# Entry of the in-projection: x also laid out by channel, u formed on VectorE instead of transposed on TensorE

## The chip, the cores and the metric

The kernel runs on one core of one Trainium2 chip. Its time is the device time of one launch in microseconds (us), from inputs in device memory to the output there. Below, TensorE is PE in the rows, VectorE is DVE, ScalarE is ACT, GpSimd is POOL and SyncE is SP; SyncE issues most of the DMAs.

## The reference, cut to what matters

Two transformer blocks run one after the other on 1024 tokens of width 1024, all in float32. What the change touches is the first line of the first block: the RMS norm of the input and the product with `w_in`.

```python
def rms_norm(x, g):
    xf = x.astype(jnp.float32)
    y = xf * lax.rsqrt(jnp.mean(xf * xf, axis=-1, keepdims=True) + EPS)
    return (y * g.astype(jnp.float32)).astype(x.dtype)
...
        u = rms_norm(h, attn_pre_norm[i])
        c_q, c_kv, k_rope, m_q, m_k, m_v, m_o, m_i, m_f = split_cols(u @ w_in[i], IN_SIZES)
```

All that follows (latent attention, mLSTM, output projection, gated feed-forward, the second block's pool mixer and layer norm) reads this projection, directly or in turn.

## The kernel before, in words

Five programs, one for each engine, are written out by hand. Each engine runs its own in order and waits on semaphores; there is no scheduler. The order of the code is the order of the work.

A product with full float32 accuracy is made of three matmuls in a faster format (`three`, L1316 and on; the matmul itself is L1325). Each operand is split into a rounded part `_hi` and the rest `_lo`, and hi x hi, hi x lo and lo x hi are summed in PSUM.

The projection wants u with the channels on the partitions: `u_hi` and `u_lo`, 128 partitions x 8 channel blocks (k) x 1024 tokens. x lies in memory by token. The entry brings it there in token tiles of 128 (t = 0 to 7), and the first weight tile is multiplied in token quarters of 256 (q = 0 to 3, two tiles each):

- SyncE loads the rows of tiles 0 and 1, the first weight tile in two halves, then tiles 2 to 7, then small tables, and later the second weight tile.
- ScalarE (`x_norm`, L1939) squares a tile with a running sum and takes the root, which gives the deviation of each token (`row_sd` counts tiles).
- TensorE spreads the norm weight over all partitions at the very start (L1359: `ones` times `gain_row` into PSUM banks 2 and 3) and warms up with 14 transposes (L1362). VectorE copies the spread weight to `pre_gain` (L2644).
- VectorE (`x_scale`, L2629) takes the reciprocal and scales the tile by token and by channel, in place (`rows_ready`).
- TensorE (`x_transposed`, L1335) transposes the tile's eight channel blocks into two PSUM banks of 4 to 7 (`rows_full`). A tile from 2 on first waits until the banks' last user is through.
- ScalarE (`u_rounded`, L1948) writes `u_hi` from PSUM (`rows_hi`), and VectorE (`u_low`, L2635) writes `u_lo` as the difference (`rows_split`).
- TensorE multiplies quarter q once `rows_split` has reached 4q + 4: for each of two column halves m of the weight tile 24 matmuls of 256 columns. In quarter 0 the matmuls with the weights' high part come first (L1371, L1372), those with the low part later (L1378), since `w_lo` is still being made by GpSimd and VectorE. Between these groups stand the transposes of the next quarter's two tiles.

After the last group `in_tile(1, ...)` goes on with the second weight tile in 128x512 matmuls. From there on the kernel streams weights: SyncE loads, GpSimd, ScalarE and VectorE split and combine, TensorE multiplies.

## Time and profile before

| | us |
|---|---|
| median of 3 runs | 1821.05 (1820.62 to 1822.2) |
| the profiled execution's own time | 1821.14 |
| its span in the trace | 1819.3 |
| TensorE busy | 1795.2 |
| VectorE busy | 1405.3 |
| ScalarE busy | 686.0 |
| GpSimd busy | 1079.0 |

Times in a trace are counted from the start of the span. The page gives the busy time of each engine and the granted clock of TensorE in 40 slices; the windows give the same for any stretch. A timeline lists instructions with start, length and, in brackets, the idle time in front and what ended it. Matmuls overlap, so the length of a single one is longer than its share of a run of them: the share is read from the starts. L12 is line 12 of the kernel before.

### The profile page before, as it was taken

Reading aid. Unit: us, or ns where it says so; the run is one execution under the profiler, and the core shown is the slowest. Engines: PE = TensorE matmul, PEld = TensorE weight load, DVE = VectorE, ACT = ScalarE, POOL = GpSimd, SP = SyncE. Lnnn points to the kernel's source line nnn. Section 1 sums busy time; section 2 is a strip of 40 time slices with the busy share of each in tenths; the row PEclk is TensorE's granted clock in tenths of the full one; section 3 lists DMA queues with packets and bytes.
Section 4 is the critical chain, followed back from the end, with each engine's and each line's share of the span. In section 5 each row is a group of like instructions: output and inputs, shape, how many; then the busy total and the mean of one; then the engine's idle time right before and its main releaser. Section 6 shows DMA issues by size and latency. Waiting matters only on the chain.

```text
span 1819.3 us, 22566 instructions
## 1 busy us (share of the span) xinstructions
PE 1795.2 (99%) x8522; PEld 1500.2 (82%) x8522; DVE 1405.3 (77%) x1614; ACT 686.0 (38%) x1202; POOL 1079.0 (59%) x748
## 2 busy tenths in 40 slices
PE   8999999999999999999999999999999999999998
PEld 8888888888888888888888887888888888888877
DVE  7879866666596757676599989668888875698897
ACT  5555577852321111111243333415433343333313
POOL 4056632170259988888778876732665465567554
PEclk9999999999999999999999999999999999999999
DMA  6252310032313323143374631112332232943122
GB/s 161 84 162 56 112 46 17 17 128 93 106 45 104 116 81 116 58 151 116 104 275 176 231 128 47 47 47 105 127 116 104 105 130 79 356 176 106 73 100 93
DMA packets 126575, 204.44 MB, mean 112 GB/s; under 512 B 31986, under 2 KB 87922, under 8 KB 123011
## 3 DMA queue, kind: packets, MB, share of 16 engines
q1 hardware_dynamic: 126434, 202.93, 32.7%
q8 instruction: 68, 1.11, 0.3%
q14 instruction: 39, 0.32, 0.1%
q10 hardware_dynamic: 34, 0.07, 0.0%
HBM read 149.42 MB, written 53.04 MB: 111 GB/s over the span
## 4 chain that ended last, share of the span: by engine, by line
PE 68%; DVE 5%; POOL 3%; issue 3%; ACT 1%; DMA 0%; DVEq 0%; SPq 0%; POOLq 0%
PE ps L1325 60%; PE ps L1652 1%; PE ps L1654 1%; PE ps L1653 1%; POOL ring_lo L1188 1%; POOL ring_hi L1187 1%; DVE y L3511 1%; PE ps L1890 1%; PE ps L1891 1%; PE ps L1892 1%; DVE y L3504 0%; DVE xs_lo L3338 0%; DVE y L3233 0%; POOL y L1244 0%; PE ps L1767 0%
## 5 line engine op out<-in xcount | busy, mean ns | idle before, releaser
L1325 PE MATMUL ps<-f_hi,ring_hi 128*128 128x512 f32 x384 | 149.7, 390 | 1.2 <-POOL ring_lo L1188 1.2
L1325 PE MATMUL ps<-f_lo,ring_hi 128*128 128x512 f32 x384 | 149.4, 389 | 0.0
L1325 PE MATMUL ps<-f_hi,ring_lo 128*128 128x512 f32 x384 | 149.4, 389 | 0.0
L1259 POOL TENSOR_TENSOR ring_lo<-w_sum,ring_hi 128x512 fp32r<-128x512 f32 x60 | 94.8, 1590 | 51.2 <-ACT ring_hi L2447 51.1
L1325 PE MATMUL ps<-d_w_hi,d_hid_hi 128*128 128x512 f32 x312 | 121.7, 390 | 1.6 <-DVE y L3233 1.3
L1188 POOL TENSOR_TENSOR ring_lo<-w_sum,ring_hi 128x512 fp32r<-128x512 f32 x80 | 117.9, 1474 | 6.7
L1325 PE MATMUL ps<-d_w_hi,d_hid_lo 128*128 128x512 f32 x312 | 121.4, 389 | 0.0
L1325 PE MATMUL ps<-d_w_lo,d_hid_hi 128*128 128x512 f32 x312 | 121.4, 389 | 0.0
L2324 ACT ACTIVATE f_copy<-ps 128x512 f32<-128x512 f32 x60 | 35.3, 596 | 220.2 <-PE ps L1325 201.3
L1325 PE MATMUL ps<-xs_hi,ring_hi 128*128 128x512 f32 x256 | 100.0, 391 | 1.4 <-DVE xs_lo L3338 1.4
L1325 PE MATMUL ps<-xs_hi,ring_lo 128*128 128x512 f32 x256 | 99.6, 389 | 0.0
L1325 PE MATMUL ps<-xs_lo,ring_hi 128*128 128x512 f32 x256 | 99.6, 389 | 0.0
L1325 PE MATMUL ps<-fs_hi,ring_hi 128*128 128x512 f32 x240 | 93.5, 389 | 0.0
L1325 PE MATMUL ps<-fs_lo,ring_hi 128*128 128x512 f32 x240 | 93.4, 389 | 0.0
L1325 PE MATMUL ps<-fs_hi,ring_lo 128*128 128x512 f32 x240 | 93.4, 389 | 0.0
L1187 POOL TENSOR_SCALAR ring_hi<-w_sum 128x512 fp32r<-128x512 f32 x80 | 71.8, 898 | 32.5 <-PE ps L1325 32.0
L1187 POOL TENSOR_SCALAR ring_hi<-stage 128x512 fp32r<-128x512 f32 x38 | 33.4, 878 | 89.1 <-PE ps L1654 83.3
L1325 PEld LDWEIGHTS ps<-f_hi,ring_hi 128*128 128x128 f32 x384 | 72.1, 188 | 16.8 <-POOL ring_lo L1188 1.9
L1325 PEld LDWEIGHTS ps<-f_hi,ring_lo 128*128 128x128 f32 x384 | 72.1, 188 | 15.1
L1325 PEld LDWEIGHTS ps<-f_lo,ring_hi 128*128 128x128 f32 x384 | 72.1, 188 | 14.8
L1073 POOL TENSOR_TENSOR w_lo<-stage,w_hi 128x1024 fp32r<-128x1024 f32 x32 | 80.5, 2515 | 2.7
L1259 POOL TENSOR_TENSOR ring_lo<-stage,ring_hi 128x512 fp32r<-128x512 f32 x24 | 35.1, 1465 | 76.4 <-ACT ring_hi L2447 76.4
(542 smaller groups left out, 5792.9 us busy)
## 6 DMA issues: line engine op xcount, KB each, us to landing
d_raw<-hid_rows SPq DMA_DIRECT2D x37, 512.0 KB, 4.5
stage<-in_w_up SPq DMA_DIRECT2D x22, 512.0 KB, 4.5
wd_raw<-in_w_down SPq DMA_DIRECT2D x22, 512.0 KB, 5.6
raw_w<-in_w_gate SPq DMA_DIRECT2D x20, 512.0 KB, 4.9
stage<-in_pool_w_in SPq DMA_DIRECT2D x16, 512.0 KB, 4.9
raw_w<-in_pool_w_in SPq DMA_DIRECT2D x16, 512.0 KB, 4.8
m_rows<-u_row SPq DMA_DIRECT2D x16, 512.0 KB, 2.6
z_rows<-z_buf SPq DMA_DIRECT2D x8, 1024.0 KB, 4.1
```

Source lines behind the costliest of these rows:

```text
L1073: g.tensor_tensor(lo, stage[:, h, :], hi.bitcast(F32), ALU.subtract).then_inc(parted[h], 1)
L1187: pool_hi.do(pool, g.tensor_scalar(view(hi), src, 1.0, 0.0, ALU.mult, ALU.add))
L1188: g.tensor_tensor(view(lo), src, view(hi).bitcast(F32), ALU.subtract).then_inc(w_split, 1)
L1259: g.tensor_tensor(as_blocks(lo, src), src, as_blocks(hi, src).bitcast(F32), ALU.subtract).then_inc(w_split, 1)
L1325: last = mm(out_ap, l, r, start=(start and j == 0), stop=(stop and j == n - 1), skip_group_check=onto)
L1652: mm(o, l_hi, w_hi[s][:, c:c + HALF], start=(k == 0), stop=False)
L1653: mm(o, l_hi, w_lo[s][:, c:c + HALF], start=False, stop=False)
L1654: last = mm(o, l_lo, w_hi[s][:, c:c + HALF], start=False, stop=(k == 7))
L1890: mm(ps[:, m, :], w_hi[1][:, c:c + P], x_h, start=(k == 0), stop=False)
L1891: mm(ps[:, m, :], w_hi[1][:, c:c + P], x_l, start=False, stop=False)
L1892: last = mm(ps[:, m, :], w_lo[1][:, c:c + P], x_h, start=False, stop=(k == 3))
L2324: f(copies[:, j, :], ps[:, bank0 + bank_of[o], :], ACT.Copy).then_inc(prod_copied, 1)
```

## The change

x of the last three quarters of the tokens is handed to the kernel a second time, as `x_t`: 128 partitions (channel within its block) x 8 columns of the norm weight, and then for each quarter 8 channel blocks x 256 tokens, 3.1 MB in all. SyncE loads it in three parts, each behind the rows of its quarter, which now come as one load of two tiles. The rows are still loaded, because the sum of squares is taken over them.

For tiles 0 and 1 nothing changes but the source of the norm weight: `x_scale` reads it from PSUM in two halves of 512, and `pre_gain` and its copy are gone.

For quarters 1 to 3 nothing is transposed. VectorE (`spread_row`) makes a diagonal matrix of the reciprocals of one tile, two of them for a quarter. TensorE (`spread_columns`) multiplies it by `ones`, which puts the reciprocal of each of 256 tokens on all partitions, into the first 256 columns of PSUM bank 3. VectorE (`u_quarter`) then forms u in PSUM banks 4 to 7 with eight instructions, one a channel block: `x_t` times the norm weight's column times bank 3. ScalarE's rounding and VectorE's subtraction read it from there as before, two channel blocks of 256 tokens a time. Since bank 3 is taken, the results of quarters 2 and 3 lie in banks 2 and 3 in another order, and `c_q_raw` is copied out accordingly.

```diff
@@ -144,9 +144,11 @@
 
 
         x_nat = at("x_nat", [P, TB, D], C)
-        pre_gain = at("pre_gain", [P, D], E)
+        x_t = at("x_t", [P, KD + 3 * KD * (S // 4)], B)
+        gain_cols = x_t[:, 0:KD]
+        spread = at("spread", [P, 6 * P], E)
         gain_row = at("gain_row", [P, D], Z)
-        junk0 = at("junk0", [P, D], B + 16 * KB)
+        junk0 = at("junk0", [P, D], B + 25 * KB)
         u_hi = at("u_hi", [P, KD, S], A, F32R)
         u_lo = at("u_lo", [P, KD, S], A + 32 * KB, F32R)
@@ -652,6 +654,10 @@
             return (1 + t + 2 * e if t < 2 else 2 * t + e + 1)
 
 
+        def spread_bank():
+
+            return ps[:, 3, 0:QT]
+
         def sp_program(sp):
             def load(t, sources):
@@ -677,8 +683,11 @@
                 x_rows(t)
             for h in range(2):
                 sp.dma_start(view[h], src[h]).then_inc(staged[h], 16)
-            for t in range(2, TB):
-                x_rows(t)
+            for q in range(1, 4):
+                rows = a["x"][0, 2 * q * P:2 * (q + 1) * P, :].rearrange("(t p) n -> p t n", p=P)
+                sp.dma_start(x_nat[:, 2 * q:2 * q + 2, :], rows).then_inc(rows_in[2 * q], 16)
+                c0, c1 = KD * QT * (q - 1) + KD if q > 1 else 0, KD * QT * q + KD
+                sp.dma_start(x_t[:, c0:c1], a["x_t"][:, c0:c1]).then_inc(rows_in[2 * q + 1], 16)
 
             for j in range(4):
@@ -1334,10 +1343,8 @@
 
             def x_transposed(t):
                 pe.wait_ge(rows_ready, t + 1)
-                if t >= 2:
-                    pe.wait_ge(rows_split, 2 * (t - 2) + 2)
                 for k in range(KD):
-                    b, c = 4 + 2 * (t % 2) + k // 4, (k % 4) * P
+                    b, c = 4 + 2 * t + k // 4, (k % 4) * P
                     last = tr(ps[:, b, c:c + P], x_nat[:, t, k * P:(k + 1) * P], ident[:])
                     if k % 4 == 3:
@@ -1363,6 +1370,12 @@
             for t in range(2):
                 x_transposed(t)
             QUARTER = S // 4
+
+            def spread_columns(q):
+                pe.wait_ge(rows_ready, 2 * q + 2)
+                cs = slice((q - 1) * QUARTER, q * QUARTER)
+                mm(spread_bank(), ones[:], spread[:, cs], start=True, stop=True).then_inc(gain_spread, 1)
+
             pe.wait_ge(rows_split, 4)
             pe.wait_ge(pool_hi.sem, 2)
             for m in range(2):
@@ -1370,26 +1383,23 @@
                     w_h = wcols(0, k, m)[0]
                     mm(ps[:, m, 0:QUARTER], w_h, u_hi[:, k, 0:QUARTER], start=(k == 0), stop=False)
                     mm(ps[:, m, 0:QUARTER], w_h, u_lo[:, k, 0:QUARTER], start=False, stop=False)
-            x_transposed(2)
-            x_transposed(3)
             tile_ready(0)
             for m in range(2):
                 for k in range(KD):
                     mm(ps[:, m, 0:QUARTER], wcols(0, k, m)[1], u_hi[:, k, 0:QUARTER], start=False, stop=(k == KD - 1))
+                if m == 0:
+                    spread_columns(1)
             for j in range(2, 8):
                 q, m = j // 2, j % 2
                 pe.wait_ge(rows_split, 4 * q + 4)
-                if j == 4:
-                    pe.wait_ge(gain_spread, 3)
                 ts = slice(q * QUARTER, (q + 1) * QUARTER)
-                c = (q % 2) * QUARTER
-                last = three(ps[:, 2 * (q // 2) + m, c:c + QUARTER],
+                b, c = (m, QUARTER) if q == 1 else (q, m * QUARTER)
+                last = three(ps[:, b, c:c + QUARTER],
                              [(*wcols(0, k, m), u_hi[:, k, ts], u_lo[:, k, ts]) for k in range(KD)])
                 if q % 2 == 1:
                     last.then_inc(in_full, 1)
                 if m == 0 and q < 3:
-                    x_transposed(2 * q + 2)
-                    x_transposed(2 * q + 3)
+                    spread_columns(q + 1)
             in_tile(1, 1, 4, 4, first=True)
 
...
@@ -1949,7 +1959,13 @@
                 for j in range(2):
                     act.wait_ge(rows_full, 2 * t + j + 1)
                     f(u_hi[:, 4 * j:4 * j + 4, t * P:(t + 1) * P],
-                      ps[:, 4 + 2 * (t % 2) + j, :].rearrange("p (k n) -> p k n", k=4),
+                      ps[:, 4 + 2 * t + j, :].rearrange("p (k n) -> p k n", k=4),
+                      ACT.Copy).then_inc(rows_hi, 1)
+
+            def u_quarter_rounded(q):
+                for j in range(4):
+                    act.wait_ge(rows_full, 4 * q + j + 1)
+                    f(u_hi[:, 2 * j:2 * j + 2, q * QT:(q + 1) * QT], ps[:, 4 + j, :].rearrange("p (k n) -> p k n", k=2),
                       ACT.Copy).then_inc(rows_hi, 1)
 
             x_norm(0)
@@ -1959,15 +1975,12 @@
             x_norm(2)
             x_norm(3)
             x_norm(4)
-            u_rounded(2)
-            u_rounded(3)
             x_norm(5)
+            u_quarter_rounded(1)
             x_norm(6)
-            u_rounded(4)
-            u_rounded(5)
             x_norm(7)
-            u_rounded(6)
-            u_rounded(7)
+            u_quarter_rounded(2)
+            u_quarter_rounded(3)
 
             act.wait_ge(early_dve, 1)
...
@@ -2629,39 +2644,70 @@
             def x_scale(t):
                 dve.wait_ge(row_sd, t + 1)
                 own.do(dve, v.reciprocal(stat_c[:, t:t + 1], stat_b[:, t:t + 1]))
-                v.scalar_tensor_tensor(x_nat[:, t, :], x_nat[:, t, :], stat_c[:, t:t + 1], pre_gain[:],
-                                       ALU.mult, ALU.mult).then_inc(rows_ready, 1)
+                for n in range(2):
+                    dve.wait_ge(gain_spread, n + 1)
+                    ins = v.scalar_tensor_tensor(x_nat[:, t, half(n)], x_nat[:, t, half(n)], stat_c[:, t:t + 1], ps[:, 2 + n, :],
+                                                 ALU.mult, ALU.mult)
+                    if n == 0:
+                        own.mark(ins)
+                own.wait(dve)
+                ins.then_inc(rows_ready, 1)
 
             def u_low(t):
                 for j in range(2):
                     dve.wait_ge(rows_hi, 2 * t + j + 1)
                     ts = slice(t * P, (t + 1) * P)
                     v.tensor_tensor(u_lo[:, 4 * j:4 * j + 4, ts],
-                                    ps[:, 4 + 2 * (t % 2) + j, :].rearrange("p (k n) -> p k n", k=4),
+                                    ps[:, 4 + 2 * t + j, :].rearrange("p (k n) -> p k n", k=4),
                                     u_hi[:, 4 * j:4 * j + 4, ts].bitcast(F32), ALU.subtract).then_inc(rows_split, 1)
 
-            dve.wait_ge(gain_spread, 2)
-            v.tensor_copy(pre_gain[:], psf[:, 2 * HALF:4 * HALF]).then_inc(gain_spread, 1)
-            dve.wait_ge(gain_spread, 3)
+            def spread_row(t):
+                dve.wait_ge(row_sd, t + 1)
+                own.do(dve, v.reciprocal(stat_c[:, t:t + 1], stat_b[:, t:t + 1]))
+                v.tensor_scalar(spread[:, (t - 2) * P:(t - 1) * P], ident[:], stat_c[:, t:t + 1], None,
+                                ALU.mult).then_inc(rows_ready, 1)
+
+            def u_quarter(q):
+                dve.wait_ge(rows_in[2 * q + 1], 16)
+                dve.wait_ge(gain_spread, 2 + q)
+                dve.wait_ge(rows_split, 4 * q)
+                for k in range(KD):
+                    c = KD + (KD * (q - 1) + k) * QT
+                    ins = v.scalar_tensor_tensor(ps[:, 4 + k // 2, (k % 2) * QT:(k % 2 + 1) * QT], x_t[:, c:c + QT],
+                                                 gain_cols[:, k:k + 1], spread_bank(), ALU.mult, ALU.mult)
+                    if k % 2:
+                        ins.then_inc(rows_full, 1)
+                    else:
+                        own.mark(ins)
+                own.wait(dve)
+
+            def u_quarter_low(q):
+                ts = slice(q * QT, (q + 1) * QT)
+                for j in range(4):
+                    dve.wait_ge(rows_hi, 4 * q + j + 1)
+                    v.tensor_tensor(u_lo[:, 2 * j:2 * j + 2, ts], ps[:, 4 + j, :].rearrange("p (k n) -> p k n", k=2),
+                                    u_hi[:, 2 * j:2 * j + 2, ts].bitcast(F32), ALU.subtract).then_inc(rows_split, 1)
+
             x_scale(0)
             x_scale(1)
             u_low(0)
             u_low(1)
-            x_scale(2)
-            x_scale(3)
+            dve.wait_ge(consts, N_CONSTS)
+            spread_row(2)
+            spread_row(3)
             dve.wait_ge(pool_hi.sem, 2)
             w0 = slice(1024, 2048)
             v.tensor_tensor(w_lo[0][:, w0], stage[:, 1, :], w_hi[0][:, w0].bitcast(F32), ALU.subtract).then_inc(parted[1], 1)
-            x_scale(4)
-            u_low(2)
-            u_low(3)
-            x_scale(5)
-            x_scale(6)
-            u_low(4)
-            u_low(5)
-            x_scale(7)
-            u_low(6)
-            u_low(7)
+            u_quarter(1)
+            spread_row(4)
+            spread_row(5)
+            u_quarter_low(1)
+            u_quarter(2)
+            spread_row(6)
+            spread_row(7)
+            u_quarter_low(2)
+            u_quarter(3)
+            u_quarter_low(3)
 
             def u_rows(k):
                 if k == 3:
@@ -3626,6 +3672,8 @@
     given = {name: _np.ascontiguousarray(inputs[name]) for name in _INS}
 
     freq = _np.float32(10000.0) ** (-_np.arange(0, ROPE, 2, dtype=_np.float32) / _np.float32(ROPE))
+    x_cols = given["x"][0].T.reshape(KD, P, 4, S // 4)[:, :, 1:].transpose(1, 2, 0, 3).reshape(P, -1)
+    given["x_t"] = _np.ascontiguousarray(_np.concatenate([given["attn_pre_norm"][0].reshape(KD, P).T, x_cols], axis=1))
     given["p"] = _np.ascontiguousarray(given["p"][0, 0].T)
     given["inv_freq"] = _np.ascontiguousarray(_np.tile(freq.astype(_np.float32), 4)[:, None])
     for name, x in given.items():
```

In the rows below `w_hi_49` and `w_lo_54` are the two parts of the first weight tile. TensorE, around the low-weight part of quarter 0, before (`x_nat` rows are transposes of tiles 2 and 3; L1378 the low-weight matmuls; L1325 quarter 1):

```order
L1341 MATMUL ps<-ident,x_nat 128x128 [waits rows_split,rows_ready]
L1341 MATMUL ps<-ident,x_nat 128x128 x7
L1341 MATMUL ps<-ident,x_nat 128x128 [waits rows_split,rows_ready]
L1341 MATMUL ps<-ident,x_nat 128x128 x7
L1378 MATMUL ps<-u_hi,w_lo_54 128x256 [waits parted1,parted0]
L1378 MATMUL ps<-u_hi,w_lo_54 128x256 x15
L1325 MATMUL ps<-u_hi,w_hi_49 128x256 [waits rows_split]
```

and now:

```order
L1389 MATMUL ps<-u_hi,w_lo_54 128x256 [waits parted1,parted0]
L1389 MATMUL ps<-u_hi,w_lo_54 128x256 x7
L1377 MATMUL ps<-spread,ones 128x256 [waits rows_ready]
L1389 MATMUL ps<-u_hi,w_lo_54 128x256 x8
L1334 MATMUL ps<-u_hi,w_hi_49 128x256 [waits rows_split]
L1334 MATMUL ps<-u_lo,w_hi_49 128x256
L1334 MATMUL ps<-u_hi,w_lo_54 128x256
```

The 16 transposes are gone from in front of the low-weight matmuls, and one matmul with the diagonals of tiles 2 and 3 stands in the middle of them. Then TensorE, between the two column halves of quarter 1, before:

```order
L1325 MATMUL ps<-u_lo,w_hi_49 128x256
L1325 MATMUL ps<-u_hi,w_lo_54 128x256
L1341 MATMUL ps<-ident,x_nat 128x128 [waits rows_split,rows_ready]
L1341 MATMUL ps<-ident,x_nat 128x128 x7
L1341 MATMUL ps<-ident,x_nat 128x128 [waits rows_split,rows_ready]
L1341 MATMUL ps<-ident,x_nat 128x128 x7
L1325 MATMUL ps<-u_hi,w_hi_49 128x256 [waits rows_split]
L1325 MATMUL ps<-u_lo,w_hi_49 128x256
```

and now:

```order
L1334 MATMUL ps<-u_lo,w_hi_49 128x256
L1334 MATMUL ps<-u_hi,w_lo_54 128x256
L1377 MATMUL ps<-spread,ones 128x256 [waits rows_ready]
L1334 MATMUL ps<-u_hi,w_hi_49 128x256 [waits rows_split]
L1334 MATMUL ps<-u_lo,w_hi_49 128x256
L1334 MATMUL ps<-u_hi,w_lo_54 128x256
```

The transposes of tiles 4 and 5 have made room for one matmul; it stands behind the 24 matmuls of quarter 1's first half. The same holds for quarter 2. VectorE from the low part of the first weights on, before:

```order
L2654 TENSOR_TENSOR w_lo_54<-stage,w_hi_49 128x1024 [waits pool_hi]
L2631 RECIPROCAL cols<-cols 128x1 [waits row_sd]
L2632 SCALAR_TENSOR_TENSOR x_nat<-x_nat,cols,pre_gain 128x1024 [waits dve_own]
L2639 TENSOR_TENSOR u_lo<-ps,u_hi 128x4x128 [waits rows_hi] x4
L2631 RECIPROCAL cols<-cols 128x1 [waits row_sd]
L2632 SCALAR_TENSOR_TENSOR x_nat<-x_nat,cols,pre_gain 128x1024 [waits dve_own]
L2631 RECIPROCAL cols<-cols 128x1 [waits row_sd]
L2632 SCALAR_TENSOR_TENSOR x_nat<-x_nat,cols,pre_gain 128x1024 [waits dve_own]
L2639 TENSOR_TENSOR u_lo<-ps,u_hi 128x4x128 [waits rows_hi] x4
```

and now:

```order
L2700 TENSOR_TENSOR w_lo_54<-stage,w_hi_49 128x1024 [waits pool_hi]
L2676 SCALAR_TENSOR_TENSOR ps<-x_t,ps 128x256 [waits rows_split,gain_spread,rows_in3]
L2676 SCALAR_TENSOR_TENSOR ps<-x_t,ps 128x256 x7
L2666 RECIPROCAL cols<-cols 128x1 [waits row_sd,dve_own]
L2667 TENSOR_SCALAR spread<-ident,cols 128x128 [waits dve_own]
L2666 RECIPROCAL cols<-cols 128x1 [waits row_sd]
L2667 TENSOR_SCALAR spread<-ident,cols 128x128 [waits dve_own]
L2688 TENSOR_TENSOR u_lo<-ps,u_hi 128x2x256 [waits rows_hi] x4
L2676 SCALAR_TENSOR_TENSOR ps<-x_t,ps 128x256 [waits rows_split,gain_spread,rows_in5]
```

Where two scalings of a tile stood ahead of the four subtractions of a quarter, now stand eight products that wait for `gain_spread` (TensorE's matmul with the diagonals) and the diagonals of the quarter after.

## Rows read from the trace of the kernel before

**Rows 1.** The page, part 1: busy us and share of the span.
```profile
PE 1795.2 (99%) x8522; PEld 1500.2 (82%) x8522; DVE 1405.3 (77%) x1614; ACT 686.0 (38%) x1202; POOL 1079.0 (59%) x748
```

**Rows 2.** Windows, a stretch each; columns in the row that begins core 0.
```profile
core 0: us, PE busy (x) PEld busy (x) DVE busy (x) ACT busy (x) POOL busy (x), PEclk, DMA share, GB/s
...
12.00:14.00 2.00, 0.43 (x5) 0.19 (x3) 1.89 (x3) 2.00 (x4) 1.92 (x2) 1.00 1.02 418
43.00:225.00 182.00, 182.00 (x805) 150.69 (x805) 159.51 (x148) 97.23 (x131) 80.68 (x48) 1.00 0.33 100
1813.00:1815.00 2.00, 0.00 (x0) 0.00 (x0) 1.93 (x4) 1.24 (x2) 0.00 (x0) 1.00 0.65 262
1815.00:1817.00 2.00, 0.00 (x0) 0.00 (x0) 1.62 (x4) 0.20 (x2) 0.00 (x0) 0.96 0.00 0
1817.00:1819.30 2.30, 0.00 (x0) 0.00 (x0) 0.00 (x0) 0.00 (x0) 0.00 (x0) 0.50 0.61 228
```

**Rows 3.** Waits of TensorE, 22.3 to 225 us: total, times, longest.
```profile
PE ps L1325 <- DVE u_lo L2639: 0.5, 1, 0.5
```

**Rows 4.** Timeline of TensorE: start us, length, instructions, idle before.
```profile
2.72 3.75 PE L1359 MATMUL ps<-gain_row,ones 1*128 1x512 f32 x4 [2.72 <-POOL causal L1055]
6.40 3.25 PE L1362 MATMUL ps<-ident 128*128 128x128 f32 x14
9.44 2.94 PE L1341 MATMUL ps<-ident,x_nat 128*128 128x128 f32 x16
13.95 0.39 PE L1371 MATMUL ps<-u_hi,w_hi 128*128 128x256 f32 x1 [1.57 <-DVE u_lo L2639]
...
17.88 1.91 PE L1341 MATMUL ps<-ident,x_nat 128*128 128x128 f32 x16
19.55 2.15 PE L1378 MATMUL ps<-u_hi,w_lo 128*128 128x256 f32 x16
22.22 0.39 PE L1325 MATMUL ps<-u_hi,w_hi 128*128 128x256 f32 x1 [0.53 <-DVE u_lo L2639]
...
25.20 1.91 PE L1341 MATMUL ps<-ident,x_nat 128*128 128x128 f32 x16
...
43.07 0.40 PE L1325 MATMUL ps<-u_hi,w_hi 128*128 128x512 f32 x1
```

**Rows 5.** Timeline of VectorE.
```profile
14.36 0.17 DVE L2631 RECIPROCAL cols<-cols 128x1 f32<-128x1 f32 x1 [0.47 <-ACT cols L1942]
...
17.16 1.22 DVE L2654 TENSOR_TENSOR w_lo<-stage,w_hi 128x1024 fp32r<-128x1024 f32 x1
...
26.72 2.47 DVE L2639 TENSOR_TENSOR u_lo<-ps,u_hi 128x512 fp32r<-128x512 f32 x4
```

**Rows 6.** Timeline of ScalarE.
```profile
11.37 1.70 ACT L1951 ACTIVATE u_hi<-ps 128x512 fp32r<-128x512 f32 x3 [0.23 <-PE ps L1341]
```

**Rows 7.** Groups of VectorE: count, busy us, mean ns, idle before.
```profile
L2639 DVE TENSOR_TENSOR u_lo<-ps,u_hi 128x512 fp32r<-128x512 f32 x16 | 10.0, 682 | 3.4 <-ACT u_hi L1951 3.3
L2671 DVE TENSOR_TENSOR u_whole<-u_hi,u_lo 128x512 f32<-128x512 f32 x16 | 10.0, 685 | 0.0
...
L2981 DVE SCALAR_TENSOR_TENSOR mix<-ps,cols,mix 128x512 f32<-128x512 f32 x8 | 5.6, 746 | 0.9 <-PE ps L1511 0.8
...
L2700 DVE SCALAR_TENSOR_TENSOR ang<-turns,ang 128x256 f32<-128x256 f32 x3 | 1.3, 426 | 0.1
...
L2631 DVE RECIPROCAL cols<-cols 128x1 f32<-128x1 f32 x8 | 1.3, 158 | 0.5 <-ACT cols L1942 0.5
...
L2932 DVE TENSOR_SCALAR probs<-probs,cols 128x128 f32<-128x128 f32 x3 | 0.9, 287 | 0.1
```

**Rows 8.** Timeline of GpSimd.
```profile
10.12 2.01 POOL L1087 TENSOR_SCALAR w_hi<-stage 128x1024 fp32r<-128x1024 f32 x1
...
20.20 1.06 POOL L1072 TENSOR_SCALAR w_hi<-stage 128x1024 fp32r<-128x1024 f32 x1 [5.61 <-DMA stage<-in_w_in]
```

**Rows 9.** DMA issues: count, KB each, median us to landing.
```profile
x_nat<-in_x SPq DMA_DIRECT2D x8, 512.0 KB, 9.0
```

More of the change, by code:

```diff
@@ L1939, in x_norm @@
             def x_norm(t):
-                act.wait_ge(rows_in[t], 16)
+                act.wait_ge(rows_in[t if t < 2 else t - t % 2], 16)
                 act_own.do(act, f(junk0[:], x_nat[:, t, :], ACT.Square, accum_out=stat_a[:, t:t + 1]))
@@ L2001, in act_program @@
                 for m in range(2):
-                    act.wait_ge(in_full, 2 * n + m + 1)
-                    f(c_q_raw[:, m, half(n)], ps[:, 2 * n + m, :], ACT.Copy).then_inc(in_taken, 1)
+                    act.wait_ge(in_full, m + 1 if n == 0 else 4)
+                    rows = ps[:, m, :] if n == 0 else ps[:, 2:4, m * QT:(m + 1) * QT]
+                    dst = c_q_raw[:, m, half(n)] if n == 0 else c_q_raw[:, m, half(n)].rearrange("p (q t) -> p q t", q=2)
+                    f(dst, rows, ACT.Copy).then_inc(in_taken, 1)
             value_weights_hi(0)
```

## The prediction

> **What bounds the kernel now.** The page comes first: TensorE is busy for 99% of the span [rows 1], so whatever delays it counts in full unless something later was late anyway. The windows come next. From 43 to 225 us TensorE is busy for all of 182.00 us, and the table of waits from 22.3 to 225 us has one entry for it, 0.5 us for VectorE's `u_lo` [rows 2, 3]. So once the entry is over there is no slack on TensorE for 180 us in which a delay could vanish, and the question is when the first 512-column matmul of the second weight tile starts: 43.07 us [rows 4]. The timeline of TensorE shows the way there: gain matmuls from 2.72, warm-up from 6.40, transposes of token tiles 0 and 1 from 9.44, a wait of 1.57 us until 13.95, 32 matmuls, the transposes of tiles 2 and 3 at 17.88, 16 low-weight matmuls at 19.55, 0.53 us of waiting, then from 22.22 six groups of 24 matmuls with two more batches of transposes (25.20 and one like it), without a gap [rows 4]. VectorE is just ahead: its subtractions for quarter 2 run from 26.72 to 29.19 [rows 5], and TensorE comes to that quarter at 25.20 + 1.67 (transposes) + 2.98 (a group) = 29.85. That lead of 0.7 us is what the change touches.
>
> **What is removed.** On TensorE 48 transposes, in three batches; one batch holds it from 17.88 to 19.55, that is 1.67 us [rows 4], together 5.0 us. On VectorE one copy of the gain and six scalings of 128x1024. Added on TensorE: three matmuls `ones` x `spread`, 256 columns in full fp32. The four gain instructions (two matmuls give four) of 512 columns take 6.40 - 2.72 = 3.68 us, 0.92 each, and at half clock, as the next batch shows: 14 transposes take 9.44 - 6.40 = 3.04 us, 0.22 each, against 1.67 / 16 = 0.10 later [rows 4]. At 256 columns and full clock an instruction is a quarter of 0.92, 0.23 us, two make 0.46, and the result is out some 0.15 us after that. TensorE's own work so shrinks by 5.0 - 1.4 = 3.6 us. If VectorE could keep its lead, that would be the gain.
>
> **Why it cannot.** The order of TensorE has `spread` for quarter q+1 behind the first 24 matmuls of quarter q, and VectorE's eight products of quarter q+1 read the bank that this matmul fills. Behind them stand two reciprocal-and-spread pairs and then the four subtractions that quarter q+1's matmuls wait for. So after the spread matmul TensorE has one group (24 matmuls) to hide a whole chain of VectorE. Before, what waited at this point was transposes of rows already scaled. I work out that chain, with each duration:
> - Eight products of 128x256 with a column as scalar, one input and the output in PSUM. No row has VectorE write PSUM. Upwards: the 128x512 form with a PSUM input and a column takes 746 ns [rows 7]; half its columns fewer at about 1.04 ns each (256 columns, 270 ns) leave 0.47. Without a column, all in SBUF, 426 ns stand in the rows. A run of four subtractions of 682 ns takes 2.47 us, so neighbours overlap by 0.08 [rows 5, 7]; hence 7 x 0.39 + 0.47 = 3.2 us. The lower bound is 7 x 0.35 + 0.43 = 2.9, the upper, if reading and writing PSUM took turns and each column cost double, 3.2 + 8 x 0.27 = 5.4. I take 3.2, since the nearest row differs only in where its result goes.
> - Two pairs of reciprocal (158 ns) and 128x128 `tensor_scalar` with a column (287 ns) [rows 7]: 0.9 us. Third quarter's chain has none.
> - Four subtractions: 2.5 us, the shape in columns and bytes unchanged [rows 5]. ScalarE's roundings (0.60 us each) run beside the products, which hand over a pair every 0.8 us.
> Chain 6.6 us, against 2.9 us of matmuls that cover it.
>
> **Step by step.** (1) Start. The gain is read from PSUM, so the copy of 1.23 us goes and the rows are ready earlier, but the warm-up holds TensorE until 9.44, and of ScalarE's four roundings the last three stand back to back from 11.37 to 13.07 [rows 4, 6]. I cost this at nothing: 13.95 stays. Ends: -1.7 (then the GpSimd half of the weights, 10.12 + 2.01, would bind [rows 8]) and +0.5 (if the earlier transposes all ran at half clock). (2) VectorE's spread of tiles 2 and 3 needs ScalarE's norms, as now (14.36), and its half of `w_lo` ends near 17.3 instead of 18.38 [rows 5]: hidden. (3) TensorE: low weights for one column half from 17.88, 8 x 0.12, to 18.84; spread matmul, result at 19.45. VectorE, idle since 17.3, starts: products to 22.7, pairs to 23.6, subtractions to 26.1. Quarter 1 starts at 26.1 where it started at 22.22: +3.9. TensorE idles from 20.4, 5.7 us. (4) A period from there: first group 2.98 (25.20 - 22.22), spread 0.6, hand-over 0.05, chain 6.6: 10.2 us, to 36.3; the next without pairs 9.3, to 45.6; then two groups, 5.9, to 51.5 us. Now it is 43.07: **+8.4 us**. (5) Clock: see below, +2.1. (6) Transfers. SyncE's queue now holds 3.1 MB more before the small loads and the second weight tile. In the full stretch 12 to 14 us it moves 418 GB/s, 2.5 us per MB-sized load, and the eight row loads take 9.0 us in the median from issue to landing [rows 2, 9]. By this the first channel-wise quarter lands near 14.5 us (wanted at 19.5), the others by 20 and 25 (wanted at 29.7 and 39.9); the rows of tiles 4 and 5 land at about 17, so their norms are there by 20, wanted by VectorE's second pairs at 22.7. The second weight tile, which GpSimd takes at 20.20 [rows 8], comes some 6 us later and is parted by 35 us; TensorE wants it at 51. All hidden; if the cover went, the first would cost what it is late. (7) Behind the entry VectorE's later work (angles, sums of `u`) moves by the same 8 us and keeps its distance from TensorE.
>
> **The clock.** At the end of the run TensorE's last matmuls stop before 1813, its clock reads 1.00 until 1815, 0.96 for 1815 to 1817 and 0.50 after [rows 2]: it fell to 1.2 GHz some 4 us after the engine went idle. At the start the pace of the transposes shows the same half level, until the batch at 9.44 speeds up [rows 4]. The wait of 1.57 us before 13.95 leaves the pace alone, and from 43 to 225 us there is no pause at all. The pause made in step 3 has 5.7 us, the next two 3.7 and 2.8. At half clock the first group of quarter 1 costs up to 2.5 more and its spread 0.45; the second group lies beside VectorE. I take 2.1 of 0 to 3.0 for one fall; the upper end is a fall in each pause, 9 us. The Trainium skill, "TensorE: Matmul & The Clock Gate" (The HAM clock gate), says in my words that the slow state is the default, activity lifts it, and a pause throttles again; it speaks against this change beyond the wait itself. By it the sum is the one with this term, without it 8.4; the end of this trace agrees, and no run here yet shows it in mid-kernel.
>
> **Sum.** Profiled: 1821.14 us, of it span 1819.3, 1.84 around it; the median of the runs, 1821.05, is the same within 0.1. 1821.05 + 8.4 + 2.1 = 1831.6 us.
>
> **Rivals.**
> - The clock stays up: 1829.5. For it: the pause is only 1.6 us longer than the time to the fall seen at the end.
> - PSUM output costs double: +6.4 (three chains of 8 x 0.27), 1838; or the clock falls in every pause, 1838 to 1840. For: no row shows such a write. Against: reading PSUM costs nothing, the subtractions take 682 ns with PSUM in, and the same form all in SBUF takes 685 [rows 7].
> - Faster: TensorE's shorter work decides, 1821.05 - 3.6 = 1817.4. It needs u of the next quarter ready within the one group behind the spread matmul, a chain under 2.9 us; from about 3.8 us per chain the change breaks even. The four subtractions alone take 2.5 of that.
> - Absorbed: something after 225 us is late in both and swallows most of it, 1821 to 1824. Against: all of it hangs on the in-projection.
> - The change does no more than read the gain elsewhere in effect, the rest hidden: no change, 1821; the same rows speak against it.
>
> **Chances.** Forecast 0.52, clock up 0.19, double cost or repeated falls 0.21, absorbed or no effect 0.05, faster 0.03. Range 1827 to 1838: it holds forecast and clock-up whole and part of the dear cases. A measurement tells 0.2%, 3.6 us, from no change: faster 0.03, within 0.04, slower 0.93.
>
> **What would show it.** In the profile after: first 512-column matmul near 53 us; waits of TensorE for `u_lo` of about 6, 4 and 3 us before quarters 1 to 3; VectorE waiting for `ps` of the spread matmul three times, 2 to 4 us; products of 0.47 us; a granted clock of 0.5 in part of 25 to 32 us. Wrong if TensorE has no such waits, if the products take 0.7 us, or if later waits of TensorE shrink by 8 us.

## The result and the profile after

The changed kernel takes 1834.86 us (median of 4 runs, 1834.52 to 1836.14) against 1820.97 for the kernel before: the ratio is 1.0074, with a 95% interval from 1.0061 to 1.0086. It is 13.9 us slower. A second set of runs, taken with the last experiments, gave the same ratio, 1.0074 (1.0061 to 1.0088). I had forecast 1831.6, and 1827 to 1838.

The page of the profile after; the first line beside [rows 1]:

```profile
span 1833.1 us, 22510 instructions
## 1 busy us (share of the span) xinstructions
PE 1797.2 (98%) x8480; PEld 1501.5 (82%) x8480; DVE 1402.8 (77%) x1639; ACT 686.8 (37%) x1202; POOL 1076.3 (59%) x748
```

The span has grown by 13.8 us, and TensorE is busy for 2 us more, not 3.6 less. The timeline of TensorE, the lines that answer to [rows 4] (L1384 is quarter 0's first matmul, L1334 those of quarters 1 to 3 and of the second weight tile, L1377 a spread matmul):

```profile
13.05 0.39 PE L1384 MATMUL ps<-u_hi,w_hi 128*128 128x256 f32 x1 [1.97 <-DVE u_lo L2660]
...
25.10 0.58 PE L1334 MATMUL ps<-u_hi,w_hi 128*128 128x256 f32 x1 [5.61 <-DVE u_lo L2688]
...
30.07 0.60 PE L1377 MATMUL ps<-spread,ones 128*128 128x256 f32 x2
...
37.22 0.58 PE L1334 MATMUL ps<-u_hi,w_hi 128*128 128x256 f32 x1 [3.69 <-DVE u_lo L2688]
...
42.51 1.00 PE L1377 MATMUL ps<-spread,ones 128*128 128x256 f32 x2
...
49.28 0.39 PE L1334 MATMUL ps<-u_hi,w_hi 128*128 128x256 f32 x1 [2.90 <-DVE u_lo L2688]
...
56.62 0.40 PE L1334 MATMUL ps<-u_hi,w_hi 128*128 128x512 f32 x1
```

Quarters 1, 2 and 3 start at 25.10, 37.22 and 49.28, each after a pause that a `u_lo` ends. The first matmul of 512 columns comes at 56.62 us, where it came at 43.07. From it to the end of the span there are 1776.5 us, and 1776.2 in the kernel before. So the whole difference is made in the entry, and nothing behind it takes any of it back. The waits of TensorE from 10 to 60 us (total, times, longest) beside [rows 3]:

```profile
PE ps L1334 <- DVE u_lo L2688: 12.2, 3, 5.6
PE ps L1384 <- DVE u_lo L2660: 2.0, 1, 2.0
```

and of VectorE for the spread matmuls:

```profile
DVE ps L2676 <- PE ps L1377: 12.2, 2, 6.4
```

Each engine waits for the other. TensorE waits for VectorE's `u_lo` ahead of quarters 1, 2 and 3 (5.6, 3.7 and 2.9 us). VectorE waits for TensorE's L1377 ahead of quarters 2 and 3 (5.7 and 6.4 us), and once more ahead of quarter 1: the view puts those 2.58 us down to "issue", but the products start at 18.64, just behind the end of the spread matmul (17.95 + 0.60). That both totals are 12.2 is chance. VectorE's timeline for quarter 1, from the first product (L2676) on, beside [rows 5]:

```profile
18.64 3.23 DVE L2676 SCALAR_TENSOR_TENSOR ps<-x_t,ps 128x256 f32<-128x256 f32 x8 [2.58 <-issue]
21.78 0.16 DVE L2666 RECIPROCAL cols<-cols 128x1 f32<-128x1 f32 x1
21.97 0.28 DVE L2667 TENSOR_SCALAR spread<-ident,cols 128x128 f32<-128x128 f32 x1
22.17 0.15 DVE L2666 RECIPROCAL cols<-cols 128x1 f32<-128x1 f32 x1
22.36 0.29 DVE L2667 TENSOR_SCALAR spread<-ident,cols 128x128 f32<-128x128 f32 x1
22.57 2.48 DVE L2688 TENSOR_TENSOR u_lo<-ps,u_hi 128x512 fp32r<-128x512 f32 x4
30.76 3.23 DVE L2676 SCALAR_TENSOR_TENSOR ps<-x_t,ps 128x256 f32<-128x256 f32 x8 [5.72 <-PE ps L1377]
```

Products, two pairs, subtractions: 18.64 to 25.05, then nothing until the next spread matmul is through at 30.7. The windows (columns as in [rows 2]; the granted clock is the number in front of the DMA share) show the third part:

```profile
20.00:22.00 2.00, 0.00 (x0) 0.00 (x0) 1.96 (x7) 1.44 (x4) 0.00 (x0) 1.00 1.05 430
22.00:24.00 2.00, 0.00 (x0) 0.00 (x0) 1.97 (x6) 1.97 (x5) 0.00 (x0) 0.71 1.00 281
24.00:26.00 2.00, 0.90 (x4) 0.90 (x5) 1.04 (x2) 1.01 (x3) 0.00 (x0) 0.50 1.27 178
...
28.00:30.00 2.00, 2.00 (x13) 2.00 (x12) 0.00 (x0) 0.00 (x0) 2.00 (x1) 0.58 0.74 6
...
36.00:38.00 2.00, 0.78 (x3) 0.78 (x4) 1.17 (x2) 0.00 (x0) 0.00 (x0) 0.63 0.71 240
38.00:40.00 2.00, 2.00 (x12) 2.00 (x11) 0.00 (x0) 0.00 (x0) 0.00 (x0) 0.50 0.00 1
...
50.00:54.00 4.00, 4.00 (x24) 4.00 (x23) 3.83 (x10) 1.69 (x4) 0.00 (x0) 0.57 0.02 4
```

The clock falls to 0.50 in the first pause, is back near 29.7, falls again in the second near 36.5, and a last time near 50.2, just after quarter 3 has begun. The first group of quarter 1 takes 30.07 - 25.10 = 4.97 us instead of 2.98.

### The profile page after: what moved, and what is told of

It is laid out like the page before. It is cut to its first block, busy times and chain, and to the rows that moved or that the text cites. A ratio compares the mean times of both kernels' runs of the same rounds, so it can differ in the third digit from the quotient of the medians.

```text
span 1833.1 us, 22510 instructions
## 1 busy us (share of the span) xinstructions
PE 1797.2 (98%) x8480; PEld 1501.5 (82%) x8480; DVE 1402.8 (77%) x1639; ACT 686.8 (37%) x1202; POOL 1076.3 (59%) x748
## 4 chain that ended last, share of the span: by engine, by line
PE 67%; DVE 5%; POOL 3%; issue 3%; ACT 1%; DMA 0%; DVEq 0%; SPq 0%; POOLq 0%
PE ps L1334 60%; PE ps L1662 1%; PE ps L1664 1%; PE ps L1663 1%; POOL ring_lo L1197 1%; POOL ring_hi L1196 1%; DVE y L3557 1%; PE ps L1900 1%; PE ps L1901 1%; PE ps L1902 1%; DVE y L3550 0%; DVE xs_lo L3384 0%; DVE y L3279 0%; POOL y L1253 0%; PE ps L1777 0%
## 5 line engine op out<-in xcount | busy, mean ns | idle before, releaser
L1334 PE MATMUL ps<-f_hi,ring_hi 128*128 128x512 f32 x384 | 149.7, 390 | 1.3 <-POOL ring_lo L1197 1.3
L1334 PE MATMUL ps<-f_lo,ring_hi 128*128 128x512 f32 x384 | 149.4, 389 | 0.0
L1334 PE MATMUL ps<-f_hi,ring_lo 128*128 128x512 f32 x384 | 149.4, 389 | 0.0
L1334 PE MATMUL ps<-d_w_hi,d_hid_hi 128*128 128x512 f32 x312 | 121.6, 390 | 1.6 <-DVE y L3279 1.3
L1334 PE MATMUL ps<-d_w_hi,d_hid_lo 128*128 128x512 f32 x312 | 121.4, 389 | 0.0
L1334 PE MATMUL ps<-d_w_lo,d_hid_hi 128*128 128x512 f32 x312 | 121.4, 389 | 0.0
L1334 PE MATMUL ps<-xs_hi,ring_hi 128*128 128x512 f32 x256 | 100.0, 391 | 1.4 <-DVE xs_lo L3384 1.4
L1334 PE MATMUL ps<-xs_hi,ring_lo 128*128 128x512 f32 x256 | 99.7, 389 | 0.0
L1334 PE MATMUL ps<-xs_lo,ring_hi 128*128 128x512 f32 x256 | 99.6, 389 | 0.0
L1334 PE MATMUL ps<-fs_hi,ring_hi 128*128 128x512 f32 x240 | 93.4, 389 | 0.0
L1334 PE MATMUL ps<-fs_lo,ring_hi 128*128 128x512 f32 x240 | 93.4, 389 | 0.0
L1334 PE MATMUL ps<-fs_hi,ring_lo 128*128 128x512 f32 x240 | 93.4, 389 | 0.0
L1334 PEld LDWEIGHTS ps<-f_hi,ring_hi 128*128 128x128 f32 x384 | 72.1, 188 | 16.9 <-POOL ring_lo L1197 1.9
L1334 PEld LDWEIGHTS ps<-f_hi,ring_lo 128*128 128x128 f32 x384 | 72.1, 188 | 15.1
L1334 PEld LDWEIGHTS ps<-f_lo,ring_hi 128*128 128x128 f32 x384 | 72.1, 188 | 14.8
```

The costliest lines, as they stand in the source:

```text
L1334: last = mm(out_ap, l, r, start=(start and j == 0), stop=(stop and j == n - 1), skip_group_check=onto)
```

## The experiments

Theory: (a) the spread matmul stands behind a group of the quarter before, so that VectorE's chain begins late; (b) the pauses so made drop TensorE's clock. Rivals: the amount of VectorE's work is the bound wherever it stands; the added loads hold the entry back.

**Spread matmuls of quarters 2 and 3 first (on the changed kernel).**

```diff
             for j in range(2, 8):
...
                 pe.wait_ge(rows_split, 4 * q + 4)
+                if m == 0 and q < 3:
+                    spread_columns(q + 1)
...
-                if m == 0 and q < 3:
-                    spread_columns(q + 1)
```

> Edit on the changed kernel: the spread matmuls of quarters 2 and 3 stand ahead of the first group of 24 matmuls of the quarter before, not behind it; nothing else. Theory (the late start of VectorE's chain costs the time): VectorE's chain now has two groups to hide behind. Quarter 1 still starts at 25.1 us; spread and two groups, partly at half clock, take about 9, quarter 2 starts near 34, its spread and groups take 6.4 and are followed at once by quarter 3, which ends near 46.5 instead of 56.6: 1825 us (1823 to 1827). Rival A (the amount of VectorE's work is the bound, wherever it stands): no gain, 1833 to 1835. Rival B (the added loads hold the entry back): no gain either, and waits on DMA in front of the products.

Measured: 1825.46 us, ratio 1.0024 to the kernel before (1.0015 to 1.0033). TensorE's waits in front of the quarters, and its first 512-column matmul:

```profile
PE ps L1377 <- DVE u_lo L2688: 6.3, 2, 5.6
```

```profile
47.65 0.40 PE L1334 MATMUL ps<-u_hi,w_hi 128*128 128x512 f32 x1
```

Of three pauses the first is left (5.6 us), the others are 0.7 and none. Moving two matmuls gives back 9.1 us of the 13.5 (by the ratios, 0.0050 of 1821), and VectorE does exactly the work that it did. Not all of it is waiting: with two pauses gone, two falls of the clock are gone too, and the profile has a single stretch at half level, from 24.0 to 30.8 us. Rival A falls. The loads are the same, so the 9.1 us are not theirs; what they cost by themselves is measured below. Two of the ten runs took 1828.1 and 1829.0 us, 3 us more than the others; no profile shows why.

**Pauses filled (on the changed kernel).**

```diff
             for j in range(2, 8):
                 q, m = j // 2, j % 2
+                if j in (2, 4):
+                    for _ in range(48 if j == 2 else 32):
+                        tr(ps[:, 2, 0:P], ident[:], ident[:])
+                elif j == 6:
+                    pe.wait_ge(rows_full, 16)
+                    for _ in range(20):
+                        tr(ps[:, 3, 0:P], ident[:], ident[:])
```

> Edit on the changed kernel: TensorE fills its three pauses with transposes of the identity into PSUM columns that nobody reads (48 before quarter 1, 32 before quarter 2, 20 before quarter 3 after the products are out). Theory (the clock's fall costs about 6 of the 13.9 us, the pauses themselves the rest): granted clock 1.00 from 10 to 57 us, groups of 24 matmuls in 2.9 us, first 512-column matmul near 50.5 instead of 56.6, 1828.8 us (1827.5 to 1830). Rival (the clock follows something else than TensorE's pauses, or the groups would be waiting anyway): 1833 to 1835 with the clock still at 0.5 in places.

Measured: 1830.7 us, ratio 1.0051 (1.0035 to 1.0066), just above the range expected. The windows:

```profile
10.00:14.00 4.00, 2.17 (x17) 1.94 (x16) 2.81 (x6) 3.85 (x8) 2.59 (x2) 0.96 1.02 423
14.00:18.00 4.00, 4.00 (x24) 4.00 (x24) 1.71 (x4) 2.01 (x6) 0.00 (x0) 0.62 1.02 420
18.00:23.00 5.00, 5.00 (x44) 4.94 (x44) 2.56 (x7) 2.64 (x7) 0.00 (x0) 1.00 1.03 415
23.00:30.00 7.00, 6.64 (x58) 6.40 (x57) 3.77 (x10) 3.60 (x8) 2.10 (x2) 1.00 0.94 137
...
37.00:44.00 7.00, 6.26 (x50) 6.17 (x50) 3.28 (x9) 1.31 (x3) 0.00 (x0) 1.00 0.12 41
```

```profile
52.93 0.40 PE L1334 MATMUL ps<-u_hi,w_hi 128*128 128x512 f32 x1
```

From 18 us on the clock is up, and it stays so. By the two ratios the fill gives back 0.0023 of the time, 4.2 us. It would be more had the clock not been at half level for a stretch before 18 us in this execution: quarter 0's 40 matmuls up to the spread took 19.75 - 13.36 = 6.4 us instead of the 4.9 of the changed kernel (17.95 - 13.05). And one diagonal of VectorE took 1.00 us here instead of 0.29 (why, see under "Quarter 1's spread matmul early"):

```profile
33.90 1.00 DVE L2674 TENSOR_SCALAR spread<-ident,cols 128x128 f32<-128x128 f32 x1
```

With both, 4.2 + 1.5 + 0.7, the clock's share is about 6.4 us; without them 4.2 are measured. That falls of the clock cost time is shown for the whole, since TensorE does more here, waits for the same chain and is yet faster.

**The loads alone (on the kernel before).**

```diff
-            for t in range(2, TB):
-                x_rows(t)
+            for q in range(1, 4):
...
+                sp.dma_start(x_nat[:, 2 * q:2 * q + 2, :], rows).then_inc(rows_in[2 * q], 16)
...
+                sp.dma_start(x_t[:, c0:c1], a["x_t"][:, c0:c1]).then_inc(rows_in[2 * q + 1], 16)
```

(ScalarE waits for the pairs accordingly, and VectorE waits for `x_t` once, behind the last subtraction of the entry.)

> Edit on the kernel before: only the loads of the change. The rows of tiles 2 to 7 come in pairs, each pair followed by its part of x_t (3.1 MB in all), which nothing reads. Theory: 1821 us (1820.5 to 1822), with ScalarE waiting for rows near 15 us and GpSimd starting the second weight tile near 27 instead of 20.2 us, and no new wait on TensorE over 1 us. Rival B (transfers): 1823 to 1830, with TensorE waiting for the quarter whose rows are late.

Measured: 1822.06 us, ratio 1.0000 (0.9991 to 1.0009). TensorE's waits, and GpSimd's start on the second weight tile [rows 8]:

```profile
PE ps L1375 <- DVE u_lo L2643: 1.6, 1, 1.6
PE ps L1345 <- DVE x_nat L2636: 0.9, 2, 0.5
PE ps L1329 <- DVE u_lo L2643: 0.5, 1, 0.5
```

```profile
28.36 1.05 POOL L1076 TENSOR_SCALAR w_hi<-stage 128x1024 fp32r<-128x1024 f32 x1 [13.52 <-DMA stage<-in_w_in]
```

The second tile comes 8 us later and nobody minds. The waits are those of before but for 0.9 us in front of the first transposes, and these are not the loads': the rows were there, and VectorE's scaling of tile 0 took 2.10 us beside GpSimd's rounding, where it takes 1.28 in the kernel before:

```profile
8.53 2.10 DVE L2636 SCALAR_TENSOR_TENSOR x_nat<-x_nat,cols,pre_gain 128x1024 f32<-128x1024 f32 x1
8.51 1.05 POOL L1089 TENSOR_SCALAR w_hi<-stage 128x1024 fp32r<-128x1024 f32 x1 [4.25 <-DMA stage<-in_w_in]
```

Rival B is worth nothing that can be measured; the interval leaves room for 1.6 us.

**The norm weight from PSUM alone (on the kernel before).**

```diff
-            dve.wait_ge(gain_spread, 2)
+            x_scale(0)
+            x_scale(1)
             v.tensor_copy(pre_gain[:], psf[:, 2 * HALF:4 * HALF]).then_inc(gain_spread, 1)
             dve.wait_ge(gain_spread, 3)
-            x_scale(0)
-            x_scale(1)
```

(`x_scale` of tiles 0 and 1 as in the change, in two halves from PSUM.)

> Edit on the kernel before: only the norm weight's part. Tiles 0 and 1 are scaled with the weight read from PSUM in halves of 512, and the copy to pre_gain stands behind them, for tiles 2 to 7. Theory (that part alone brings the first multiplications forward): they start near 13.0 to 13.3 us instead of 13.95, and all behind them by the same, 1820.2 us (1819.7 to 1820.8). Rival (my prediction's view: ScalarE's roundings or the warm-up hold the start anyway): start at 13.9, 1821.0 us. Side reading: GpSimd's two roundings of 128x1024 take 1.04 us each instead of 2.1 and 2.0 where VectorE reads one operand from PSUM beside them.

Measured: 1821.08 us, ratio 0.9996 (0.9987 to 1.0005): no decision by the times. TensorE's start, and GpSimd's two roundings:

```profile
2.39 3.75 PE L1359 MATMUL ps<-gain_row,ones 1*128 1x512 f32 x4 [2.39 <-DMA gain_row<-in_attn_pre_norm]
...
13.28 0.39 PE L1371 MATMUL ps<-u_hi,w_hi 128*128 128x256 f32 x1 [1.96 <-DVE u_lo L2649]
```

```profile
7.76 1.05 POOL L1085 TENSOR_SCALAR w_hi<-stage 128x1024 fp32r<-128x1024 f32 x1 [3.50 <-DMA stage<-in_w_in]
9.19 1.05 POOL L1087 TENSOR_SCALAR w_hi<-stage 128x1024 fp32r<-128x1024 f32 x1 [0.38 <-DMA stage<-in_w_in]
```

The gain matmul, whose start depends on when its DMA lands, begins at 2.39 here and at 2.72 before; counted from it quarter 0 starts after 10.89 us instead of 11.23 [rows 4]. The start came where it was expected, but the part is worth 0.3 us, not the 0.9 that I read off the start of the changed kernel. It matches a wait in the kernel before, of the weight loads of tile 1's transposes for VectorE's scaling, which is not there in this run:

```profile
11.28 0.86 PEld L1341 LDWEIGHTS ps<-ident,x_nat 128*128 128x128 f32 x8 [0.33 <-DVE x_nat L2632]
```

Another 0.3 us is the later gain matmul of before. The rest, 0.25 us, lies in the sixteen transposes: they take 1.95 us in the changed kernel and 2.21 here. I take that to be the point at which the clock rose, which I have not tested. The side reading came out: the roundings take 1.05 us, where the second took 2.01 [rows 8].

**Quarter 1's spread matmul early (on the changed kernel).**

```diff
                     mm(ps[:, m, 0:QUARTER], w_h, u_lo[:, k, 0:QUARTER], start=False, stop=False)
+                if m == 0:
+                    spread_columns(1)
...
-                if m == 0:
-                    spread_columns(1)
```

> Edit on the changed kernel: the spread matmul of quarter 1 stands in the middle of quarter 0's high-weight matmuls, once its diagonals are there, not behind the first eight low-weight ones; nothing else. Theory: VectorE's products for quarter 1 begin near 16.1 instead of 18.6 us and quarter 1 starts at 22.6 instead of 25.1; TensorE's first pause is 3.1 us instead of 5.6. 2.5 us less from the start itself, and up to 2.5 more where the clock does not fall in that pause: 1830 to 1832.5 us. Rival (the first hand-over is not what sets quarter 1's start; row loads or norms do): 1834 to 1835.

Measured: 1834.54 us, ratio 1.0068 (1.0055 to 1.0082): not the 1830 to 1832.5 expected, and only 1.1 us below the changed kernel on the same chip (1835.67, the last run), with intervals that overlap. Quarter 1 does start 2.3 us earlier (22.87 - 2.25 = 20.6 us after the gain matmul, against 25.43 - 2.56 = 22.9 in the second run of the changed kernel). But TensorE's next pause grew to 5.6 us: the clock fell in three stretches again (the first time near 24.0, when quarter 1 had run for 1.2 us), and in the next chain a diagonal that takes 0.29 us elsewhere took 2.17. VectorE's row and GpSimd's beside it:

```profile
31.76 2.17 DVE L2667 TENSOR_SCALAR spread<-ident,cols 128x128 f32<-128x128 f32 x1
```

```profile
31.45 2.40 POOL L1082 TENSOR_TENSOR w_lo<-stage,w_hi 128x1024 fp32r<-128x1024 f32 x1
```

It ends when GpSimd's operation ends, at 33.9. The second chain, being earlier, had come to lie under GpSimd's work on the second weight tile. The same shows in other traces: in the first experiment two diagonals of this chain took 1.18 and 0.91 us, with pauses filled one took 1.00, and with the loads alone VectorE's scaling, started 0.02 us behind a rounding of GpSimd's, took 2.10. Each time the one that starts second is held. That such a pair excludes each other I read from these rows; I have made no run to test it by itself. That it and the clock together are why the 2.5 us did not appear is argued from this one profile.

**All spread matmuls ahead (on the changed kernel).** The first stands behind quarter 0's first 16 matmuls, the second ahead of quarter 1, the third behind it.

```diff
-        def spread_bank():
-
-            return ps[:, 3, 0:QT]
+        def spread_bank(q):
+
+            return ps[:, 2 if q == 2 else 3, 0:QT]
...
+                if m == 0:
+                    spread_columns(1)
...
-                if m == 0:
-                    spread_columns(1)
+            spread_columns(2)
...
-                if m == 0 and q < 3:
-                    spread_columns(q + 1)
+                if j == 3:
+                    spread_columns(3)
```

> Edit on the changed kernel: all three spread matmuls stand ahead. Quarter 1's in the middle of quarter 0's high-weight matmuls, quarter 2's (into PSUM bank 2) ahead of quarter 1, quarter 3's behind quarter 1's two groups. Theory: quarter 1 starts at 22.6, VectorE never waits for a spread matmul, its chain of 6.6 us a quarter runs beside 5.9 to 6.4 us of TensorE, and the first 512-column matmul is near 41 us against 43.1 in the kernel before: 1819 us (1818 to 1820) with the clock up; a fall in the first pause of 3 us adds up to 3, 1822. Rival A (VectorE's amount of work bounds it anyway): above 1825.

Measured: 1820.39 us, ratio 0.9992 (0.9983 to 1.0001): no difference from the kernel before that the runs can tell, and Rival A (above 1825) is out. VectorE's wait for a spread matmul, TensorE's for `u_lo` behind quarter 0, and its first 512-column matmul:

```profile
DVE ps L2677 <- PE ps L1377: 1.6, 1, 1.6
```

```profile
PE ps L1334 <- DVE u_lo L2689: 1.7, 1, 1.7
```

```profile
42.76 0.40 PE L1334 MATMUL ps<-u_hi,w_hi 128*128 128x512 f32 x1
```

VectorE's 12.2 us of waiting have become 1.6, and of TensorE's three pauses the first is left with 1.7. The clock was at half level from 24.0 to 27.4 us in this execution, which is most of why 41 became 42.8.

**The same with two pauses filled (on the last).**

```diff
+            for _ in range(14):
+                tr(ps[:, 0, 0:P], ident[:], ident[:])
             pe.wait_ge(rows_split, 4)
...
             spread_columns(2)
+            for _ in range(18):
+                tr(ps[:, 3, 0:P], ident[:], ident[:])
```

> Edit on e4_spread_ahead: two pauses of TensorE filled with transposes of the identity that nobody reads, 14 ahead of quarter 0 and 18 ahead of quarter 1. Theory (what is left of the pauses can still drop the clock, in some executions even the one of 1.8 us ahead of quarter 0): clock 1.00 throughout, 1818.5 to 1819.5 us with less spread than e4_spread_ahead. Rival (transposes get in the way of the real work): 0.5 to 1 us above e4_spread_ahead.

Measured: 1819.64 us (1819.09 to 1820.12 over 11 runs), ratio 0.9988 (0.9979 to 0.9997), 0.1 us above the range expected and with the smaller spread. It beats both kernels, the one before by 2.1 us; the interval, 0.5 to 3.8 us, just leaves out no difference. TensorE's waits for the diagonals, its first 512-column matmul and the window of the entry (clock 1.00):

```profile
PE ps L1377 <- DVE spread L2672: 0.7, 2, 0.5
```

```profile
41.75 0.40 PE L1334 MATMUL ps<-u_hi,w_hi 128*128 128x512 f32 x1
```

```profile
10.00:57.00 47.00, 46.23 (x311) 42.51 (x310) 43.33 (x90) 23.75 (x45) 10.14 (x6) 1.00 0.61 169
```

**The changed kernel again.**

> The changed kernel as it is, on the same chip as the two versions with the spread matmuls ahead. Theory: 1834.9 us, the clock at half level in three stretches before 57 us, in the profiled execution and by the times in all others. Rival (the falls depend on the execution's phase): times spread over several us between 1829 and 1837.

Measured: 1835.67 us, 1834.98 to 1835.99, ratio 1.0074. In its profile the clock falls in the same three places and the 512-column matmuls begin at 57.20. The four times lie within 1 us, so in this kernel the falls come every time as far as two profiles and eight times tell.

In all these runs the stretch from the first 512-column matmul to the end of the span is the same: 1776.0 to 1776.9 us, for example 1818.0 - 41.75 in the fastest version and 1834.1 - 57.20 in the last run.

## Why the prediction was right, and by how much not

- *No slack behind the entry*: right. 1776.2 us before and 1776.5 after, in every experiment within 0.5 us of 1776.4. The rival "absorbed" is out.
- *The chain begins behind a group of 24*: right, in place and size. From VectorE's first product to quarter 1's first matmul 25.10 - 18.64 = 6.46 us, 6.6 forecast. The first experiment takes the late start away and gets 9.1 us back, the clock's part in it included.
- *Products 3.2 us from the row with a column and PSUM in*: right, 3.23 us, one of them 484 ns against 470 forecast. The rival of double price is out (its +6.4 should read 6.5). Pairs and subtractions as forecast (0.8 and 2.48).
- *Start costed at nothing*: quarter 0 began 0.9 us earlier, within the bounds; 0.3 us of it belong to the change. The step overlooked the 0.33 us that the transposes of tile 1 had to wait for VectorE's scaling.
- *Transfers hidden*: right. Rows of tile 4 at 16.7 (17 forecast), GpSimd's start on the second weight tile at 26.85 (20.20 and some 6 us forecast), and the loads alone cost nothing measurable.
- *VectorE's waits for the spread matmuls*: forecast three of 2 to 4 us, measured 2.6, 5.7 and 6.4. The last two are longer because the group and the spread matmul in front of them ran at half clock.
- *+8.4 us without the clock*: quarter 1 was due at 26.1 and came at 25.10. The periods, without what the half clock added (about 2.0, 2.8 and 1.5 us), are 10.1, 9.3 and 5.8 us, against 10.2, 9.3 and 5.9. The sum of the chain holds.
- *Clock +2.1*: the term that was too small. I priced one fall and kept three for the upper end. They came in both profiled executions (and by the times in the others), and cost 2.0 + 2.8 + 1.5 = 6.3 us by the groups, 4.2 to 5.7 by the filled pauses. With what held up the filled version otherwise, 1.5 and 0.7 us, the second figure is 6.4. I had measured the pauses, forecast at 5.7, 3.7 and 2.8 us, against the 4 us from the last matmul to the fall [rows 2], as though that were what it takes. The clock fell around shorter ones too. The rows of before could not show that: their one short pause, 1.57 us, left the clock up.
- *The case that came*: the wait is the one that I forecast, but with three falls of the clock, which I had put into another case (double cost or repeated falls, 0.21, at 1838 to 1840), not into the forecast at 0.52. That the time stayed in the range all the same is partly luck: a fall cost 1.5 to 2.8 us where I had allowed 3, and quarter 0 began 0.9 us early.
- *Faster*: out of reach in this order. With the spread matmuls ahead and two pauses filled the kernel is 2.1 us faster than the one before, of the 3.6 us that TensorE was to save; in the profiles the first 512-column matmul comes 1.3 us earlier (41.75 against 43.07).

Together: 8.4 us forecast without the clock, less the 1.0 us by which quarter 1 came early, and 6.3 for the clock make 13.7 us; the span grew by 13.8.

## What to carry to other kernels

When a step on one engine is replaced by a hand-over between two, look first where the other's instruction stands in its queue: work that is cheaper on both engines is slower when its request stands behind the work it is to hide under. Issue the request ahead of the cover, with a buffer of its own. And price pauses of TensorE like those here (2.9 to 5.6 us) as the pause and then much of the next group at half speed, unless matmuls that nobody reads fill them. Last, see what another engine does at the new time of a chain: in three experiments VectorE's chain grew by 0.7 to 1.9 us when VectorE's diagonals came to lie beside GpSimd's work.

## What the runs showed of the hardware that was not expected

- TensorE's granted clock fell to 0.5 in runs where its pauses were short, and in several falls matmuls had begun again. In the filled version it read 0.96 for 10 to 14 us and 0.62 for 14 to 18, after a pause of 1.8 us ahead of quarter 0; in the changed kernel a pause of 2.0 us at the same place left it at 1.00. With all spread matmuls ahead it fell near 24.0 us, 0.8 us behind the end of a pause of 1.7. In the changed kernel the third fall, near 50.2 us, came 0.9 us after matmuls had begun again. What decides which short pause drops the clock stays open here. The Trainium skill, "TensorE: Matmul & The Clock Gate" (The HAM clock gate), puts it that the point at which the clock rises varies from run to run with the gate's own phase. The pace of the sixteen transposes of tiles 0 and 1 agrees with that: they took 1.95 us in one profile of the changed kernel and 2.15 in the other.
- GpSimd's `tensor_scalar` of 128x1024 takes 1.04 us in these two rows of the changed kernel, where VectorE reads one operand from PSUM beside it:

```profile
7.67 1.04 POOL L1094 TENSOR_SCALAR w_hi<-stage 128x1024 fp32r<-128x1024 f32 x1 [3.41 <-DMA stage<-in_w_in]
9.12 1.04 POOL L1096 TENSOR_SCALAR w_hi<-stage 128x1024 fp32r<-128x1024 f32 x1 [0.41 <-DMA stage<-in_w_in]
```

  In the kernel before, beside VectorE's scaling with both operands in SBUF, the second took 2.01 [rows 8]. The other way round VectorE's 128x128 `tensor_scalar` was held until GpSimd's `tensor_tensor` had ended, 2.17 us instead of 0.29, and VectorE's scaling behind a rounding took 2.10 instead of 1.28.
- VectorE writes PSUM at the price that I had worked out from rows with an SBUF output: 128x256 with a column and one PSUM input, eight in 3.23 us against 3.2. No run has this very form with its output in SBUF.
